# The first tile's output projection: from the front of the second tile's mixer to the end of its own

## The reference

```python
        u = u_tab[idx]
        h = jax.nn.gelu(jnp.einsum('bthkd,btd->bthk', u, xi).astype(jnp.float32), approximate=False)
        w = (gate * h).astype(xi.dtype)
        return jnp.einsum('bthk,bthkd->btd', w, v_tab[idx])
...
    proj = h @ w_in
    cb, cc, cu, q, k, v, f_logit, g_conv, g_att = split_cols(proj)
    y_conv = short_conv(cb, cc, cu, conv_w, conv_b) @ w_conv_out
...
    y_att = o.reshape(B, S, D_ATT) @ w_att_out
    m = jax.nn.sigmoid(g_conv) * y_conv + jax.nn.sigmoid(g_att) * y_att
    return m @ w_out
```

## Time and profile before

| what | value |
|---|---|
| times of three runs | 2441.65, 2443.19, 2444.59 us (median 2443.19) |
| the profiled execution | 2444.95 us, its span from first to last instruction 2443.1 us |
| TensorE, VectorE, GpSimd busy | 1983.3, 1099.2, 978.9 us |
| read from HBM | 904 MB, 371 GB/s over the span |

### The profile page before, as it was taken

The page is one execution under the profiler, slowest core; times in us unless marked ns, Lnnn a source line. Parts: engine busy times, 40 slices in busy tenths (PEclk is TensorE's granted clock), DMA queues, the critical chain, the costliest instruction groups (busy, mean ns, idle before and its releaser), DMA issues.

```text
span 2443.1 us, 22115 instructions
## 1 busy us (share of the span) xinstructions
PE 1983.3 (81%) x7920; PEld 1014.6 (42%) x7920; DVE 1099.2 (45%) x2663; ACT 439.8 (18%) x1123; POOL 978.9 (40%) x1059
## 2 busy tenths in 40 slices
PE   8927997679989778998878999999999875665554
PEld 5523553235445225445324664444685432222221
DVE  6579647963466964465975343344211210000001
ACT  2312411111311111311111111232102210000000
POOL 0036765674656776555777544555000000000000
PEclk9968998999999999999999999999999978788887
DMA  6278999999999999999999999999895579999996
GB/s 225 95 267 330 408 409 409 398 409 405 409 389 401 409 409 409 405 407 371 409 409 409 409 409 409 410 409 409 294 388 201 207 293 427 426 428 427 427 427 260
DMA packets 217921, 906.97 MB, mean 371 GB/s; under 512 B 27840, under 2 KB 28352, under 8 KB 206032
## 3 DMA queue, kind: packets, MB, share of 16 engines
q0 software_dynamic: 147456, 536.94, 55.6%
q1 hardware_dynamic: 67088, 358.77, 36.9%
q10 hardware_dynamic: 3264, 9.80, 1.0%
HBM read 904.37 MB, written 1.05 MB: 371 GB/s over the span
## 4 chain that ended last, share of the span: by engine, by line
PE 41%; DMA 27%; DVE 18%; POOL 7%; issue 5%; ACT 1%; SPq 1%; DVEq 0%; ACTq 0%; POOLq 0%
PE psum L2075 12%; DMA rows<-in_peer_v,idx 11%; PE psum L1874 9%; PE psum L1882 7%; DVE rows L1075 6%; DMA rows<-in_w_e_gate 5%; DMA rows<-in_w_e_down 4%; DMA rows<-in_w_e_up 3%; POOL rows L728 3%; POOL rows L716 3%; PE psum L2238 3%; DMA rows<-in_peer_u,idx 3%; PE psum L1843 2%; PE psum L2261 1%; DVE work L958 1%
## 5 line engine op out<-in xcount | busy, mean ns | idle before, releaser
L2075 PE MATMUL psum<-rows,diag 128*128 128x512 f32 x2024 | 969.5, 622 | 195.0 <-ACT diag L1581 105.0
L1075 DVE CUSTOM_DVE_ANT_0 rows<-rows,psum 128x1024 f32<-128x1024 f32 x512 | 614.7, 1219 | 417.5 <-DMA rows<-in_peer_u,idx 405.1
L2075 PEld LDWEIGHTS psum<-rows,diag 128*128 128x128 f32 x2024 | 377.1, 196 | 722.6 <-issue 506.4
L728 POOL DMA_INDIRECT rows<-in_peer_v,idx x512 | 487.4, 952 | 378.2 <-PE psum L2075 261.2
L716 POOL DMA_INDIRECT rows<-in_peer_u,idx x512 | 487.7, 953 | 363.6 <-DVEq L753 142.3
L1874 PE MATMUL psum<-rows,work 128*128 128x512 f32 x544 | 238.5, 593 | 2.1 <-ACT work L1400 2.1
L1882 PEld LDWEIGHTS psum<-work,rows 128*128 128x128 f32 x1920 | 219.4, 193 | 13.2 <-issue 9.8
L1882 PE MATMUL psum<-work,rows 128*128 128x128 f32 x1920 | 220.0, 276 | 3.1 <-DMA rows<-in_w_in 3.1
L1400 ACT ACTIVATE work<-psum 128x512 f32<-128x512 f32 (+5 forms) x190 | 95.5, 516 | 697.5 <-PE psum L1882 218.9
L1581 ACT ACTIVATE diag<-ident,wgt 128x128 f32<-128x128 f32 x506 | 167.4, 389 | 283.2 <-DVE wgt L1083 283.2
L1341 DVE TENSOR_TENSOR work<-kept,psum 128x512 f32<-128x512 f32 x8 | 8.2, 1031 | 425.4 <-PE psum L2238 425.4
(11 more groups left out here) (305 smaller groups left out, 1388.5 us busy)
## 6 DMA issues: line engine op xcount, KB each, us to landing
rows<-in_w_in SPq DMA_DIRECT2D x64, 1024.0 KB, 9.8
rows<-in_w_e_up SPq DMA_DIRECT2D x28, 2048.0 KB, 22.2
rows<-in_w_e_down SPq DMA_DIRECT2D x25, 2048.0 KB, 22.1
rows<-in_w_e_gate SPq DMA_DIRECT2D x24, 2048.0 KB, 24.4
rows<-in_gla_w_in SPq DMA_DIRECT2D x24, 1024.0 KB, 9.3
rows<-in_peer_w_query SPq DMA_DIRECT2D x16, 1024.0 KB, 9.3
rows<-in_peer_u,idx POOLq DMA_INDIRECT x512, 10.4
rows<-in_peer_v,idx POOLq DMA_INDIRECT x512, 10.5
```

Source lines behind the costliest of these rows:

```text
L728: pool.indirect_dma_start(out=v_rows[:, n % RV, :], out_offset=None, in_=a["peer_v"][g // 2], in_offset=bass.IndirectOffsetOnAxis(ap=idx[: ...
L1075: V_.tensor_tensor_reduce(out=u, in0=u, in1=tokens, scale=1.0, scalar=0.0, op0=ALU.mult, op1=ALU.add, accum_out=hid[:, r:r + 1]).then_inc( ...
L2075: last = mm(psum[:, 6 + c, :], diag[:, at % DIAGS, :], v_rows[:, n % RV, c * BANK:(c + 1) * BANK], start=r == 0, stop=summed(n + 1) == sum ...
```

## The change

The job p moves from the front of `mix(1)` to the end of `mix(0)`, on all engines that have a part in it, and gets four counts of rows for each of its two jobs. Where it stood on TensorE, 14 products without use (`idle`, ones by the mask, 128x256, into bank 4) are put. The pieces of `w_out` keep their place in `PIECES`; only the stage that they belong to is another. The banks of p are now 3 and 0 instead of 4 and 5.

```diff
     if stage == "mix":
         jobs = (["x0", "x1", "f"] + [f"{m}{i}" for m in ("cc", "cu", "cb", "q", "k", "v") for i in range(2)]
                 + attention_jobs(v, BETWEEN) + turned_jobs(v) + ["ya0", "ya1", "mT0", "mT1"])
-        return ["p0", "p1"] + jobs + ["o0", "o1", "x00", "x01", "r0"] if v else jobs
+        return jobs + (["o0", "o1", "x00", "x01", "r0"] if v else ["p0", "p1"])
...
-        streamed = [m for m in TWO_BANKS["mix"] if m not in ("p", "o")]
+        streamed = [m for m in TWO_BANKS["mix"] if m != "o"]
         return {"x1": 2, "f": 2, "oT0_1": 2, "mT1": 2,
                 **{f"{m}{i}": 4 for m in streamed for i in range(2)},
...
-        out = pair("w_out", "p1") if v else []
-        out += [("mix_gain", 0, D, "x1"), ("w_in_2", 6 * D, FH, "f")]
+        out = [("mix_gain", 0, D, "x1"), ("w_in_2", 6 * D, FH, "f")]
...
-        return out + pair("w_out", "o1") if v else out
+        return out + pair("w_out", "o1" if v else "p1")
...
-                    got(key, "p1")
+                    got(("mix", 0), "p1")
                     link(V_.tensor_tensor(h[:, 0, :], h[:, 0, :], x_out, ALU.add))
...
-                if t:
-                    row_major("p", x_out)
                 by_feature("x", x_xT)
...
                 by_feature("mT", x_mT)
+                if t == 0:
+                    row_major("p", x_out)
...
-            def idle(n):
+            def idle(n, bank=7):
                 for _ in range(n):
-                    mm(psum[:, 7, 0:2 * P], ones[:], mask[:], start=True, stop=True)
+                    mm(psum[:, bank, 0:2 * P], ones[:], mask[:], start=True, stop=True)
...
                 if t:
                     pe.wait_ge(u_used, NU)
-                    got(("mix", 0), "mT1")
-                    pair(key, both("p"), x_mT)
+                    idle(14, XB)
                 seen(key, "xn")
...
                 if t == 0:
                     seen(key, "m1")
                     transposes(key, "mT1", chunks(x_ya, 1))
+                    got(key, "mT1")
+                    pair(key, both("p"), x_mT)
                     return
```

## The result

The changed kernel takes 2446.51 us (median of 20 runs) against 2444.37 us of the kernel before (median of 20 runs); the ratio is 1.0015 with a 95% interval of 1.0009 to 1.0022. By the interval that is a loss of 2 to 5 us. The time is inside the predicted range and the ratio inside 0.2% (the upper end of its interval is not), but it is on the slower side of the 2443.5 us forecast.

What follows compares the result with a forecast made beforehand. Row gathers (DMA) bound the kernel until p, TensorE from 1745 us; "xn" at 1743.87 puts the transposes at 1743.9 against 1743.60, so 2443.19 + 0.3 = 2443.5 us, range 2438.5 to 2448.5.

Steps and rivals of the forecast that it cites:

- Place and price of p: Second mixer's front loses the 6.81 us beyond the norm; p amid the last rows ends TensorE's last row 7.46 us later.
- ScalarE's diagonals behind the copies of p: Diagonals of rows 504 to 510 follow p's two copies, ending near 1729.6; TensorE needs row 504's at 1730.35: no cost.
- The gather of row 511: Last gather, issued after row 502 at 1730.63, lands 5.8 us later; VectorE adds at 1737.75, 0.2 us behind TensorE.
- the forecast's own range: 2441.7 (no 1.2 GHz stretch behind the second weight wait) to 2446.6 us (row 511 lands 8.9 us after issue); chance 0.74.
- The rival of the last gather: Row 511, queued with weight pieces, lands after 13.1 us and ends the rows: 2450.8 us; chance 0.11.
- Idle products at no cost: Before the transposes, 28 idle records take 6.05 us, under the 6.12 us of add and norm; 3.5 us at lower clock.
- The row of 22 records in 7.54 us: Idle records at program start, taken as partly at 1.2 GHz; gave 9.6 us for 28 records, 3.5 us on the path.
- The early weights give nothing: In the projections both weight waits (1.08 and 1.97 us) recur: no gain; rival that they count: 2438.7 us, chance 0.10.
- the 1.8 of the prediction: Cost in us of the 1.2 GHz stretch behind the projections' second weight wait: 160 records in 19.76 against 17.96 us.
- TensorE's idle time takes p whole: Rival: rows end at 1730.03 as before, transposes begin at 1736.84, 6.8 us gained: 2436.4 us; chance 0.05.

Runs made afterwards that it cites:

- row 502 first: The changed kernel with row 502 moved ahead of p's second half, six counts of rows instead of four in p's middle: 2443.18 us, ratio to before 1.0003.
- half of p: Against the changed kernel, only p's first half amid the rows, its second half under VectorE's add and norm, no idle products: 2437.38 us, ratio to before 0.9982.
- 22 idle products: The changed kernel with 22 idle products instead of 14 in front of the transposes: 2446.61 us, ratio to before 1.0013.
- no idle products: The kernel with SP's first second-mixer weights held until all rows are used, without its 14 idle products: 2445.08 us, ratio to before 1.0011.
- weights after the rows: The changed kernel, but SP issues the second mixer's first weights (f and cc) only when all rows are used: 2443.50 us, ratio to before 1.0006.
- half of p, weights after the rows: Changed kernel with p's second half under the norm, no idle products, and second-mixer weights held until all rows are used: 2438.43 us, ratio to before 0.9983.

## Why the prediction was right, and where it was not

- **Place and price of p: right.** The front lost what stood beyond the norm, and the rows gained 7.5 us: TensorE's last row ends 35.75 us behind the mark, 1737.50 by the prediction's clock, where the prediction had 1737.49. A sum of records at 0.429 us was enough.
- **ScalarE's diagonals behind the copies of p: right,** without cost; there is no gap in the 20 records behind p.
- **The gather of row 511: the step that failed, in one term.** The issue is on the spot (29.15 behind the mark; predicted 1730.63 - 1701.75 = 28.88). The landing was taken as 5.8 us, the quickest gather plus 1.3 us for an equal share of the DMA; it was 8.3. The quickest gather was a good base (4.68 us alone, 4.5 taken), and the equal share held while both moved: 0.52 MB of the row beside 0.42 MB of weights. Two things were missing: the row began to move 1.4 us later, behind the weights of which 1.01 MB passed from 1735 to 1738, and moving cost 2.2 us more than alone and not 1.3. From the issue until the row had landed 1.38 MB of weights moved, 3.4 us at 409 GB/s; the quickest gather plus that would have been 7.9 us, an estimate after the fact, from this one case. In the forecast's own range this case stood with 8.9 us and 2446.6 us. The rival of the last gather was right in its mechanism (a row that sets the end, and weights ahead of it), and not in its size, since it decides only from 10.4 us on.
- **Idle products at no cost: right only as long as "xn" comes 6.1 us behind the last row.** It came 9.2 us behind it. The prediction priced idle products that end too late, not ones that end too early. That is a second term that was missing, 1.2 us by the clock; the run with 22 of them shows its cause, and the run without any shows it again behind a longer wait, with 2.5 us. (The row of 22 records in 7.54 us, which the prediction takes for partly at 1.2 GHz, has a granted clock of 1.00 in the trace; 9.6 us for 28 is not shown by it.)
- **The early weights give nothing: right in this profile.** The waits in the projections are 0.45 + 2.54 = 3.0 us, against 3.05; from cc to v it is the same to 0.1 us. It is not sure for every execution: with row 502 first, which has the same early weights, the waits are 2.6 us, no stretch at 1.2 GHz follows, and from cc to v it takes 75.2 us instead of 76.8. That stretch costs 1.6 us and not the 1.8 of the prediction, which took the tail off one row and not off the other.
- **TensorE's idle time takes p whole: not so** as placed; the rule of the Trainium skill ("Perfetto Trace Analysis", section "Optimization Strategy"), that interleaving stages with different limits may help, agrees with the run of half of p: there 3.5 us are gained at the transposes. The idle time of the rows took 3.7 us of the first half's 6.9, and the second half lay under the norm.

In the sum: predicted +0.3 us to the start of cc, measured in the profile +4.4. Of the difference 2.8 are the later add (2.5 of the landing, 0.3 of the issue), and 1.2 the clock. In the time the change costs 2.1 us by the medians and 3.7 by the ratio. So the forecast is right by its range and its class, not by its sum; and that 2446.51 lies so close to the slow end of its range from 2441.7 to 2446.6 is in part luck, since the kernel before took 2444.37 us beside it and not the 2443.19 from which the forecast starts.

## What to carry to other kernels

Work that is moved beside a stage bound by transfers costs nothing only up to that stage's idle time; the rest makes its end later, and whatever covered a wait at the old place has to be covered again. Split such work by the idle time on either side before adding filler. When a moved step also frees buffers, look at which transfers this starts, and whether a late transfer that ends the stage will queue behind them.

## What the runs showed of the hardware

- One gather of 128 rows of 4 KB, issued with two pieces of 1 MiB in flight, was with its reader 7.1 us (22 idle products) and 8.3 us (changed kernel) after its issue; with no other transfer in flight 4.3 (no idle products) and 4.7 us (weights after the rows). Behind other gathers and without weights it was 6.1 us (half of p, weights after the rows) and 8.9 us (before). In the changed kernel its packets began 3.0 us after the issue, alone 1.6; while it moved it had 23.6% of the engines and the weights 24.3%, near the even share of two long streams.
- Behind a wait of TensorE of 3.23 us a part of the transposes and of f ran at 1.2 GHz (the granted clock of that stretch was 0.60), behind one of 6.39 us all of both (0.50). Where idle products of 128x256 filled the time (row 502 first, weights after the rows, 22 idle products), the same work ran at 2.4 GHz, 3.6 to 3.7 us to cc instead of 4.9 and 6.2.
- The mark, behind rows that are the same in all kernels, lay between 1700.7 and 1706.0 us in eight profiled executions. A comparison of two profiles of this kernel needs a mark just ahead of the change.
